# Hybrid decoder layer on one core: a head's decays come to all partitions by a transfer from a scratch tensor, are masked on GpSimd, and the flag of the first gather is raised earlier

## Time and profile before

| | |
|---|---|
| median of 3 runs | 1495.82 us (1495.68 to 1497.97) |
| the profiled execution | 1496.73 us |
| its span, first to last instruction | 1494.9 us |
| PE busy | 1366.7 us, 91% of the span, 7772 matmuls |
| DVE busy | 614.2 us, 41% |
| ACT busy | 438.2 us, 29% |
| POOL busy | 58.0 us, 4% |
| granted TensorE clock, mean | 0.978 |
| DMA | 480.02 MB, mean 321 GB/s |
| head stage, of the span | from 71 to 405 us |
| output projection and routing | 405 to 535 us |
| experts | 535 to 1484 us |

### The profile page before, as it was taken

How to read it: one execution, slowest core, us unless ns; L and a number is a source line. 1 busy time by engine, 2 the same in 40 slices (tenths; PEclk the granted TensorE clock), 3 DMA queues, 4 the chain that set the end, 5 groups by cost and what they waited for, 6 DMA issues and landing times.

```text
span 1494.9 us, 20440 instructions
## 1 busy us (share of the span) xinstructions
PE 1366.7 (91%) x7772; PEld 838.4 (56%) x7772; DVE 614.2 (41%) x1144; ACT 438.2 (29%) x865; POOL 58.0 (4%) x57
## 2 busy tenths in 40 slices
PE   5999999999999979899899899899899899989985
PEld 3899999999877843353343343343343345335332
DVE  5877777777855531212212222222132123221323
ACT  5455655656534621111111121111111111102112
POOL 0011110111100000000000000000000000000000
PEclk9999999999999989999999999999999999999998
DMA  7735555455625659999999999999999999999994
GB/s 201 196 93 144 142 140 144 116 144 144 201 91 176 256 234 406 427 428 427 428 429 428 429 428 428 428 428 427 429 428 428 429 429 429 429 429 419 427 429 178
DMA packets 145879, 480.02 MB, mean 321 GB/s; under 512 B 11241, under 2 KB 111794, under 8 KB 120626
## 3 DMA queue, kind: packets, MB, share of 16 engines
q1 hardware_dynamic: 145842, 479.50, 82.2%
HBM read 477.39 MB, written 2.10 MB: 321 GB/s over the span
## 4 chain that ended last, share of the span: by engine, by line
PE 68%; DMA 22%; DVE 6%; ACT 2%; issue 2%; SPq 1%; DVEq 0%; ACTq 0%
PE bank L547 66%; DMA ew<-in_expert_w_dram 22%; PE bank L550 2%; DVE w_parts L1422 1%; ACT ew L1334 1%; DVE fw L1880 1%; DMA fw<-in_norm_ffn_w_dram 0%; SPq L514 0%; ACT fw_r L1261 0%; DVE fw L1686 0%; DVE ew L1461 0%; DVE ew L1888 0%; DVE fw_r L1741 0%; DVE fw L1382 0%; ACT ew L1336 0%
## 5 line engine op out<-in xcount | busy, mean ns | idle before, releaser
L547 PE MATMUL bank<-ew,hT 128*64 128x512 f32 (+1 forms) x1568 | 464.4, 600 | 40.0 <-DMA ew<-in_expert_w_dram 33.6
L547 PEld LDWEIGHTS bank<-ew,hT 128*64 128x64 f32 (+1 forms) x1568 | 155.5, 141 | 336.0 <-issue 335.8
L547 PE MATMUL bank<-act_parts,w_parts 128*128 128x256 f32 x2304 | 307.8, 288 | 1.7 <-DVE w_parts L1422 1.7
L547 PEld LDWEIGHTS bank<-act_parts,w_parts 128*128 128x128 f32 x2304 | 284.9, 191 | 2.9 <-issue 1.4
L547 PE MATMUL bank<-ew 128*64 128x512 f32 (+2 forms) x1120 | 252.1, 581 | 6.9 <-DVE ew L1890 6.9
L547 PE MATMUL bank<-mixT,hT 128*64 128x512 f32 x512 | 225.4, 593 | 0.0
L1888 DVE SCALAR_TENSOR_TENSOR ew<-ew,bank 128x256 f32<-128x256 f32 x32 | 13.5, 421 | 452.5 <-ACT ew L1336 452.5
L547 PEld LDWEIGHTS bank<-ew 128*64 128x64 f32 (+1 forms) x1120 | 85.5, 143 | 150.1 <-issue 139.8
L1422 DVE TENSOR_TENSOR w_parts<-fw,w_parts 128x2048 fp32r<-128x2048 f32 x64 | 147.5, 2309 | 28.2 <-ACT w_parts L1025 27.0
L1351 ACT ACTIVATE ye_r<-bank 64x512 fp32r<-64x512 f32 x128 | 68.8, 585 | 283.1 <-PE bank L547 282.3
L1334 ACT ACTIVATE ew<-bank,gs 128x512 f32<-128x512 f32 x32 | 22.0, 687 | 420.5 <-PE bank L547 420.5
(11 more groups left out here) (244 smaller groups left out, 1057.7 us busy)
## 6 DMA issues: line engine op xcount, KB each, us to landing
ew<-in_expert_w_dram SPq DMA_DIRECT2D x160, 2048.0 KB, 16.4
mixT<-in_expert_w_dram SPq DMA_DIRECT2D x32, 2048.0 KB, 17.9
fw<-in_w_in_dram SPq DMA_DIRECT2D x48, 1024.0 KB, 5.9
fw<-in_w_out_dram SPq DMA_DIRECT2D x16, 1024.0 KB, 5.1
mixT<-in_x_dram SPq DMA_DIRECT2D x1, 2048.0 KB, 7.6
fw<-in_x_dram SPq DMA_DIRECT2D x1, 2048.0 KB, 10.1
out_dram<-fw SPq DMA_DIRECT2D x4, 512.0 KB, 2.7
fw<-in_norm_final_w_dram SPq DMA_DIRECT2D x1, 1024.0 KB, 19.5
```

The source lines that it names most:

```text
L547: return nc.tensor.matmul(o, l, r, start=start, stop=stop, skip_group_check=True)
```

## The change

- `rows` (16 x 384) is written once to a scratch tensor `decay_rows` in HBM by SyncE, which waits for that transfer, and then for each head row h + 8 of it is read with a partition step of 0 into `gb`, 128 x 384 in SBUF (`load_decay`). For head 0 this stands behind the first head's loads; for head h it stands behind the third piece of head h, with a wait for `s_D` at h.
- GpSimd adds the mask to the first and third vector of `gb` in place (`decay_mask`), for head 0 ahead of its other work, for head i + 1 behind head i's six multiplications. Its two bfloat16 copies at the start go.
- ScalarE's `decays` reads `gb` in place of bank 6 and waits for GpSimd; for head 0 it also waits for the copy of the bias columns (`s_prm` at 2).
- `select`, `decay_rows` and their semaphores go, and TensorE's wait for `s_mix` moves from level 5 to behind level 6.
- The memset that raises `s_turn` moves from behind the gate factors to behind the last addition (`add_last(1)`).

```diff
-        bigm = sb("bigm", [P, P], BF16)
-        idb = sb("idb", [P, P], BF16)
-        rsel = sb("rsel", [16, 3, P])
+        gb = R1b.take(3, P)
+        rows_d = nc.dram_tensor("decay_rows", (16, 3 * P), F32, kind="Internal").ap()
...
             load_rg(0)
+            def load_decay(h):
+                sp.dma_start(gb.rearrange("p a b -> p (a b)"),
+                             rows_d[bass.ds(h + NH, 1), :].broadcast_to([P, 3 * P])).then_inc(s_gb, 16)
+
+            sp.wait_ge(s_barow, 2)
+            sp.dma_start(rows_d, rows.rearrange("p a b -> p (a b)")).then_inc(s_rows, 16)
+            sp.wait_ge(s_rows, 16)
+            load_decay(0)
             with sp.Fori(1, NH) as h:
                 for b in range(6):
                     slot_free(h * 6 + b)
                     load_block(h, b)
+                    if b == 2:
+                        sp.wait_ge(s_D, h)
+                        load_decay(h)
...
-            def decay_rows(h):
-                pe.wait_ge(s_sel, h + 1)
-                mm(bank[6][:, 0:3 * P], cst[0:16, C_ONE:C_ONE + P], rsel[:, :, :].rearrange("p a b -> p (a b)"),
-                   True, False)
-                mm(bank[6][:, 0:P], idb[:, :], bigm[:, :], False, False)
-                mm(bank[6][:, 2 * P:3 * P], idb[:, :], bigm[:, :], False, True).then_inc(s_gb, 1)
...
-                    if lv == 5:
-                        if last_done:
-                            pe.wait_ge(s_mix, h * 2)
-                        if nxt is not None:
-                            decay_rows(nxt)
                 pe.wait_ge(s_X, h * (LEVELS - 1) + LEVELS - 1)
                 pe.wait_ge(s_vt, h + 1)
+                if last_done:
+                    pe.wait_ge(s_mix, h * 2)
...
-            pe.wait_ge(s_mask, 1)
             pe.wait_ge(s_barow, 1)
             keys(0)
-            decay_rows(0)
             gates(0)
...
-                act.wait_ge(s_gb, h + 1)
+                act.wait_ge(s_gbm, h + 1)
                 for q, bias in ((0, Q_NG), (1, Q_OFF), (2, Q_NG + 1)):
-                    l = act.activation(Dk[:, q], bank[6][:, q * P:(q + 1) * P], ACT.Exp, bias=pc[:, bias:bias + 1])
+                    l = act.activation(Dk[:, q], gb[:, q], ACT.Exp, bias=pc[:, bias:bias + 1])
...
-            act.wait_ge(s_sel, 1)
+            act.wait_ge(s_prm, 2)
             decays(0)
...
-            def select(h):
-                if not (isinstance(h, int) and h == 0):
-                    dve.wait_ge(s_gb, h)
-                V.tensor_scalar(rsel[:, :, :], rows[:, :, :], cst[0:16, bass.ds(h + (C_SEL + NH), 1)], None, ALU.mult).then_inc(s_sel, 1)
...
-            link(V.tensor_copy(pc[:, Q_NG:], prm[:, Q_NG:, 0]))
-            select(0)
+            V.tensor_copy(pc[:, Q_NG:], prm[:, Q_NG:, 0]).then_inc(s_prm, 1)
+            dve.wait_ge(s_prm, 2)
...
-                        select(i)
                         silu(i, 0)
...
             add_last(1)
+            V.memset(cnt[:, 2:3], 0.0).then_inc(s_turn, 1)
             route(0)
...
             gates_of(0).then_inc(s_gq0, 1)
-            V.memset(cnt[:, 2:3], 0.0).then_inc(s_turn, 1)
...
-            G.tensor_copy(bigm[:, :], cst[:, C_BIG:C_BIG + P])
-            G.tensor_copy(idb[:, :], ident).then_inc(s_mask, 1)
+            big = cst[:, C_BIG:C_BIG + P].rearrange("p (a i) -> p a i", a=1).broadcast_to([P, NT, P])
+
+            def decay_mask(h):
+                pool.wait_ge(s_gb, h * 16 + 16)
+                G.tensor_tensor(gb[:, 0:3:2, :], gb[:, 0:3:2, :], big, ALU.add).then_inc(s_gbm, 1)
+
+            decay_mask(0)
             G.tensor_copy(tri_one[:, :], cst[:, C_TRI:C_TRI + 2 * P]).then_inc(s_tri, 1)
-            with pool.Fori(0, NH) as i:
+            with pool.Fori(0, NH - 1) as i:
                 heads(i)
+                decay_mask(i + 1)
+            heads(NH - 1)
```

More of the change, by code:

```diff
@@ L340, in build @@
         s_gate = sem("s_gate")
-        s_sel = sem("s_sel")
+        s_rows = sem("s_rows")
+        s_gbm = sem("s_gbm")
         s_gb = sem("s_gb")
```

## The result

The changed kernel takes 1487.7 us, the median of 6 runs (1485.76 to 1490.62), against 1495.88 us (1495.68 to 1498.89, 6 runs) for the kernel before. The ratio is 0.9941, with a 95% interval of 0.9928 to 0.9954: 8.2 us less, where 8.8 were predicted. The profiled execution took 1486.90 us, 9.8 less than the profiled one of before.

What follows compares the result with a forecast made beforehand. TensorE bounds the head loop, the weight stream the expert stage. 7.7 - 0.5 + 0.7 + 0.9 = 8.8 us off 1495.82 gives 1487.0 us; range 1484.0 to 1491.5, forecast as it stands 1485 to 1489.5.

Steps and rivals of the forecast that it cites:

- head 0: First head: decays start 0.9 us sooner, exponentials lose 0.14; gain 0.7 us, between 1.5 and a loss of 1.1.
- seven turns: TensorE in turns 1 to 7: removing three decay matmuls saves 1.10 us a turn, 7.7 in all; lower bound 6.4.
- last head: Start of output projection: VectorE's first operand comes 0.58 us less early than TensorE; loss 0.5 us, between 0 and 1.1.
- flag: Start of the gather: with the memset moved earlier, TensorE starts 0.93 us sooner; 0.9 us won after the memset's 0.05.
- gather and experts: Expert stage: the weight stream's start moves with TensorE, its length does not change; gains ahead come off the end.
- VectorE's debt: Each turn: VectorE up to 0.58 us late at line 1582, hidden behind projection fills, repaid from 2.23 us idle; no stall.
- the rival that VectorE becomes the bound: Head turns: VectorE or ScalarE limits each turn's gain to 0.52 us; 4.1 us less won, 1491.1 us; 13%.
- the late piece: Head 0: head 1's first weight piece, queued behind SyncE's wait, issues 5.3 us later; VectorE slips 0.8 us.
- Ready by 62 us, wanted at 71. Hidden.: Head 0: decay rows' write, read back and GpSimd's mask finish by 62 us, before they are wanted at 71.
- The Trainium skill's 2.0 us: Head 0's round trip: fixed time per GpSimd-path transfer; by it the piece goes 0.7 us sooner, gain up to 1.4.
- My rival: Head 0's gates: TensorE's clock has not yet fallen, saving about 1.5 us, 0.8 more from the piece; 1484.7 us; 7%.
- the rival that the stream swallows it: Expert stage: the stream's start is set by something other than TensorE, so the time stays at 1495.8 us; 4%.

Runs made afterwards that it cites:

- matmuls_kept: Changed kernel with the three decay matmuls put back on TensorE in each of the seven turns, their result unread: 1492.46 us.
- side_load: Changed kernel with select's multiplication put back on VectorE each turn, unread, and GpSimd's mask for heads 1 to 7 added twice: 1487.76 us.
- late_mask: Changed kernel with GpSimd adding head 0's mask only after VectorE's third silu: 1486.22 us.
- second profile: Unedited changed kernel, profiled again when timed beside two edits; median there 1486.69 us, ratio 0.9945 to the kernel before.
- flag_only: Kernel before with only the memset of the flag moved to behind the last addition: 1496.55 us.
- piece_first: Changed kernel with head 1's first weight piece issued ahead of SyncE's wait for the decay rows and their round trip: 1485.6 us; later median 1487.19.

## Why the prediction was right, and where not

**The sum.** The profiled pair, stage by stage, in us won:

| term | predicted | measured | from |
|---|---|---|---|
| head 0 | 0.7 | 0.7 | gates' first matmul 0.9 sooner (29.14 and 28.23), 0.2 lost again by the solve's first (33.59 and 32.87) |
| seven turns | 7.7 | 7.8 | from there to the idle time: 327.24 and 319.48 |
| start of the head stage | - | -0.2 | 44.33 and 44.53, outside the change |
| last head | -0.5 | -0.25 | idle 3.56 and 3.81 |
| clock behind it | - | 1.0 | the next 60 matmuls: 15.17 and 14.17 |
| to the cast of `nrounds` | -0.05 | -0.1 | 108.97 and 109.05 long |
| flag | 0.9 | 0.8 | 2.32 and 1.50 |
| gather and experts | 0 | 0.0 | second freed buffer's load issued at 550.48 and 540.68, last row 940.1 later in both |
| **sum** | **8.8** | **9.8** | |

**TensorE in turns 1 to 7.** Right. The 1.10 us a turn came out (1.11 in the profiles), and `matmuls_kept` gives it back. Read from two stretches of the same sequence, with and without the matmuls, it was better than the 0.91 of their own row, which leaves out the two masks.

**VectorE's debt.** Right that it is hidden behind the fills, with one refinement: it is paid back sooner than I put it. At the very next hand-over (line 1586, now 1579) VectorE is on time again, with 0.50 us of idle time left of 1.00. What is carried on goes by way of ScalarE: ScalarE has waited 0.65 us for the late VectorE (line 1588, at 150.08), so its split comes later, and VectorE waits 1.25 us for it in place of 0.75 right behind that hand-over. Of this, 0.24 is left at line 1567, 2.23 to 1.99. The last head's idle time grew by 0.25, so the term of 0.5 was too large: I let the whole debt pass by a pause of 1.00 that stands in my own rows. That the 0.25 there is this same remainder is likely and not shown. The rival that VectorE becomes the bound is refuted by the turns of 45.95 us in which TensorE has no idle time, and `side_load` shows that there was room for more.

**Head 0.** The size was right, 0.9 us at the gates for 0.7, of which the clock took 0.2 back; the mechanism was right only by half. The round trip took 2.1 us, not 2.7, but the read back's issue took 0.7 in place of 0.4. On the common scale the piece's issue and the split came 0.3 sooner than I put them, so the split began 2.5 us later than before and not 2.8. I had VectorE wait for the late piece, 0.8 us; by `late_mask` that alone is 0.44. The slip of 0.68 in the changed kernel is GpSimd's mask and cast beside VectorE. That a slip of 0.8 was forecast and 0.68 measured is luck, since it has another cause. This is the step that failed: "Ready by 62 us, wanted at 71. Hidden." The latency of the mask was hidden; its presence on the SBUF side was not, and I looked for that only in the turns, where VectorE is idle. The new path of the decays then won what was foreseen: the exponentials follow the bias copy after 0.03 us (71.43 + 0.17 to 71.63), where before 1.7 us lay between the earlier trace rows.

The Trainium skill (GPSIMD Engine Reference, "Specifications") says that GpSimd shares its SBUF interfaces with VectorE, and that VectorE instructions with two SBUF inputs contend, as do those in a 2-port mode. The trace agrees, with 0.95 against 0.42 us; and it shows who waits. The subtraction of line 1421, in progress when the mask began, kept its 2.29 us while the mask took 1.87 instead of 0.73; the silu behind it was the one that grew. Beside the cast, line 1456 with one tensor input took 0.48 for 0.35; whether it runs in the page's 2-port mode, no run here shows.

The Trainium skill's 2.0 us (DMA: Bandwidth & Descriptors, "Anatomy of one DMA") was given for the GpSimd path. The measured 2.1 us of a 24 KB write on SyncE's queue agrees with it better than my row of 2.7, which moved 512 KB.

**The flag.** Right at the gather: 0.8 for 0.9, and the first matmul stands at 525.41, right behind its sequencer's register row at 525.3. Further on, the gather's own length varies by 1.6 us between executions with the clock's return, more than the flag wins.

**The clock.** My rival had the clock's gain in head 0. There it won nothing. The four gate matmuls took 1.49 us in place of 2.04 (2.05 in the second profile), because the clock fell after they had begun. But it came back later as well: TensorE worked for 3.4 us at the low level there, against 2.9 before, and from the gates' first matmul to the solve's first it is 4.64 us against 4.45. This is the 0.2 that head 0 lost again. The clock's gain came at the last head instead, 1.0 us, where TensorE worked for 3.4 us at the low level against 5.5 before. Whether that belongs to the change stays open. Of the ten profiles with short turns nine show 14.1 to 14.2 us for the 60 matmuls, and the three with the decay matmuls in the turns (before, `flag_only`, `matmuls_kept`) show 15.1 to 15.2; but the tenth, the same program as the first, shows 15.44. So the longer time is possible with short turns too; no run shows what decides it, and the median's 8.2 us need no gain of the clock.

**The experts.** From that issue to the last row, 13 profiles give 938.5 to 941.5 us, with no order by kernel, and 940.1 both before and after in the first pair. So what is won ahead comes off the end, and the rival that the stream swallows it is out. Those 3 us are also a good part of the spread of one kernel's runs.

**The prediction's arithmetic.** Its inner range, 1485 to 1489.5, isn't what its own bounds give. They add up to gains from 5.1 to 10.1 us, which is 1485.7 to 1490.7. The issue of the piece, 48.94 + 2.7 + 0.4, is 52.0 and not 52.1. Neither changes the forecast.

## What to carry to other kernels

To price an instruction taken off a saturated engine, find the same sequence with and without it in one trace; the difference of the distances is the price. When work moves to GpSimd, ask not only whether its result is in time, but what VectorE does in those microseconds: in a pause of VectorE the mask was free, beside it it cost 0.4 to 0.7 us wherever it was put. When a queue gets a wait, price what is queued behind it from the row of its consumer, and see how much longer it would have to be to matter; here it was 6 us more for a loss of 7.

## What the runs showed of the hardware

- One GpSimd add of 128x256 values beside VectorE: a 128x256 instruction 0.42 to 0.95 us, three conv steps 1.52 to 1.96, two of 128x8 from 0.17 each to 0.54 and 0.31 (a cast ran beside the second). The cost was 0.44 to 0.53 us in all three places, whatever the size of what the add met, and the add takes 0.73 us alone. The subtraction that was already in progress lost nothing; there the add took 1.87 us.
- Behind a pause of 3.81 us TensorE's clock fell 0.3 us after work began and came back at 3.7 in one execution; in another of the same program it fell 0.6 us before work began and came back at 6.2. The difference was worth 1.3 us. Behind head 0's gates TensorE worked at the low level for 2.9 us in the kernel before, 3.4 in the changed one and 6.1 in `late_mask`.
- A 24 KB write from SBUF to HBM with its confirmation: 2.1 us from issue to landing with nothing queued ahead of it, 4.9 behind a 1 MB read (`piece_first`); four of them in a row, each waited for, took 6.0 us, 1.5 each.
